# A second token half that starts with the weight blocks the first half ended with, and memory tokens transposed earlier

## The chip, the cores and the metric

The kernel runs on one core of one Trainium2 chip. The metric is the time of one execution on the device in microseconds. Five engines work side by side and meet through semaphores: TensorE (PE, with its weight loads as PEld), VectorE (DVE), ScalarE (ACT), GpSimd (POOL) and SyncE (SP), which here only issues the DMA transfers.

## The reference, cut to what matters

One decoder layer on 512 tokens of width 1024, all in float32. Four sub-layers, each wrapped in two RMS norms: a SwiGLU FFN, a token mixer, a cross-attention to 256 memory tokens, and a second FFN.

```
h = h + 0.5 * rmsnorm(swiglu(rmsnorm(h)))                      # FFN 1, width 2816
h = h + rmsnorm(concat(fox_attention, gla) @ w_out)            # mixer
q = rmsnorm(h) @ w_mq;  k, v = split(rmsnorm(mem) @ w_mkv)     # 4 heads of 256
o = softmax(q k^T / 16) v
h = h + rmsnorm(o @ w_mo)                                      # memory cross-attention
h = h + 0.5 * rmsnorm(swiglu(rmsnorm(h)))                      # FFN 2
```

The FoX attention has 8 heads of 64, the GLA part 4 heads in chunks of 64 tokens. The output of GLA is normed per head and gated.

## The kernel before, in words

**Products.** Every float32 product is made of three products of rounded parts: high x high, high x low, low x high (helper `three`, lines L1436, L1437, L1440). A weight block is 128 rows of 1024 values, 512 KB, or the same amount in another cut. SP fetches it into one of four slots (`raw`, L493), two transfers of 256 KB; ACT rounds it to its high part (`w_hi`, L644, in `round_block`/`round_to`); POOL subtracts to get the low part, in place of the raw block (`w_lo`, L588, in `split`); TensorE waits for the low part (`weights(n)`). SP may refill a slot when `w_used` says that the block four places earlier is finished. Blocks are numbered through the whole program: `B_OUT` begins the mixer's output weight, `B_MO` the memory output weight, `B_UP2` the second FFN.

**Row products.** A sub-layer's output is built in the eight PSUM banks: tile m is 128 tokens by 512 columns, tiles 0 to 3 are the first token half, 4 to 7 the second. `rows_block` adds one weight block to some tiles; `closing_rows` adds two blocks to each tile and so finishes the tiles one after another (`tile_done`, `w_used`). `rows_norm` on ACT (square, L691; root, L671) and DVE (sum of the two squares of a token row, L1060; weighing, L1062; `h`, L1073) norms the tiles and adds them to `h`. `turn_half` (L1513) then transposes `h` on TensorE, ACT and DVE write its high and low parts `xh` (L658) and `xl` (L1030), and `opening_pair` begins the next sub-layer with the first token half.

**Memory output.** The product with `w_mo` is made once for each token half: the first half inside the memory attention, as filling between its units, the second half after it. The eight blocks are fetched twice, 0 to 7 for each half, 16 block numbers from `B_MO`.

**Attention loops.** The FoX attention runs over 32 units (head, token tile), the memory attention over 16. In turn k TensorE makes the scores of unit k, the output of the pair that ends with unit k-3, and transposes the probabilities of unit k-2; ACT makes the exponential, then rounds weight blocks up to a number tied to the filling (`round_to`), copies out a finished output, copies the transposed probabilities (`pt_hi`, L861 and L897); DVE takes the maximum (L1209, L1211), normalises (L1140) and makes the low part (`pt_lo`, L1178 and L1220). Between these stands filling: `FILL` gives for each FoX turn how many quarters of a mixer input block TensorE puts in, `MEM_FILL` gives for each memory turn the number of items before and after the attention output. The first 16 items there are quarters of the last query blocks, the others the rows of the memory output; the last four are `closing_rows` items of two products each.

**GLA end.** After the last GLA output TensorE goes on to `fox_out(0..7)`, halves of the first four mixer output blocks, which need PSUM banks that ACT squares (L935) and DVE copies out (L1361). In between stand `sums` (L1921), the transposes of the memory tokens `mem_turn(0)` and `mem_turn(1)` (L1905), and `spread_head` (L1929), which waits for the reciprocal of the norm's root (L1363).

[...]

## Time and profile before

| | us |
|---|---|
| Median of 3 runs | 1189.07 (1186.98 to 1190.51) |
| The profiled execution's own time | 1188.42 |
| Its span in the profile | 1186.69 |
| TensorE busy in it | 1160.1 |
| ACT, POOL, DVE busy in it | 454.6, 499.4, 352.4 |

The times of rows in the next section count from the start of the span. In a row of the timeline stand: start, duration, engine, line, operation, output<-inputs, shapes, how many, and in brackets the time that the engine was idle before it and what ended that.

### The profile page before, as it was taken

The numbers are of one execution on the slowest core, as the hardware profiler recorded it, in microseconds if no ns is written. First come the engines' busy times: TensorE is split into PE (matmuls) and PEld (weight loads), VectorE is DVE, ScalarE is ACT, GpSimd is POOL, SyncE is SP. The second block draws the span as 40 slices with busy tenths as digits, with TensorE's granted clock in tenths as the row PEclk, the third lists the DMA queues.
The fourth block names the chain that finished last, engine by engine and source line by source line (L and its number), as shares of the span: only waits on it lengthen the run. The fifth ranks groups of instructions, "written<-read, shape, count | busy, mean of one in ns | idle before, by whom it ended". The sixth has DMA issues, their size and how long they took to land.

```text
span 1186.7 us, 15254 instructions
## 1 busy us (share of the span) xinstructions
PE 1160.1 (98%) x5664; PEld 965.5 (81%) x5664; DVE 352.4 (30%) x718; ACT 454.6 (38%) x744; POOL 499.4 (42%) x227
## 2 busy tenths in 40 slices
PE   8999999999999999999899999899999999999998
PEld 7888888888888778787778988778888888888886
DVE  2221311310006274655545204544122131130003
ACT  6232332322126455454535545456423233231213
POOL 5354354354443542222325754256434435435441
PEclk9999999999999999999999999999999999999999
DMA  6323333332322222111223442233332333323232
GB/s 201 105 91 99 96 94 101 92 103 89 106 89 71 89 89 72 54 54 43 83 69 109 160 142 89 73 126 107 104 105 90 98 96 92 103 89 106 89 107 107
DMA packets 86141, 115.13 MB, mean 97 GB/s; under 512 B 8974, under 2 KB 54092, under 8 KB 86092
## 3 DMA queue, kind: packets, MB, share of 16 engines
q1 hardware_dynamic: 86000, 114.44, 29.7%
q8 instruction: 33, 0.54, 0.2%
q14 instruction: 16, 0.13, 0.0%
q10 hardware_dynamic: 92, 0.02, 0.0%
HBM read 112.34 MB, written 2.10 MB: 96 GB/s over the span
## 4 chain that ended last, share of the span: by engine, by line
PE 61%; issue 24%; POOL 11%; DVE 2%; DMA 1%; ACT 1%; POOLq 0%; SPq 0%; DVEq 0%
PE bank L1436 20%; PE bank L1440 20%; PE bank L1437 20%; POOL w_lo L588 10%; PE bank L1477 1%; DVE h L1073 1%; DMA raw<-in_ffn_w_gu 1%; DVE bank L1062 0%; PE bank L1513 0%; POOL q_hi L626 0%; POOL q_lo L626 0%; DVE tmp L1062 0%; DVE f_ms L1060 0%; ACT w_hi L644 0%; ACT xh L658 0%
## 5 line engine op out<-in xcount | busy, mean ns | idle before, releaser
L588 POOL TENSOR_TENSOR w_lo<-raw,w_hi 128x1024 fp32r<-128x1024 f32 x204 | 488.3, 2403 | 665.0 <-ACT w_hi L644 664.3
L1436 PE MATMUL bank<-xh,w_hi 128*128 128x512 f32 (+1 forms) x912 | 349.8, 384 | 2.7 <-POOL w_lo L588 2.0
L1437 PE MATMUL bank<-xh,w_lo 128*128 128x512 f32 (+1 forms) x912 | 348.3, 382 | 0.0
L1440 PE MATMUL bank<-xl,w_hi 128*128 128x512 f32 (+1 forms) x912 | 348.3, 382 | 0.0
L644 ACT ACTIVATE w_hi<-raw 128x1024 fp32r<-128x1024 f32 x204 | 213.3, 1057 | 349.5 <-DMA raw<-in_ffn_w_down 167.5
L1436 PEld LDWEIGHTS bank<-xh,w_hi 128*128 128x128 f32 x912 | 171.5, 188 | 36.6 <-POOL w_lo L588 2.6
L1440 PEld LDWEIGHTS bank<-xl,w_hi 128*128 128x128 f32 x912 | 171.4, 188 | 33.6
L1437 PEld LDWEIGHTS bank<-xh,w_lo 128*128 128x128 f32 x912 | 171.5, 188 | 32.0
L1436 PE MATMUL bank<-w_hi,mid_hi 128*128 128x512 f32 x352 | 137.3, 390 | 0.0
L1440 PE MATMUL bank<-w_lo,mid_hi 128*128 128x512 f32 x352 | 137.0, 389 | 0.0
L1437 PE MATMUL bank<-w_hi,mid_lo 128*128 128x512 f32 x352 | 136.9, 389 | 0.0
L1107 DVE TENSOR_TENSOR tmp<-bank,rinv 128x512 f32<-128x512 f32 x44 | 30.2, 686 | 343.8 <-PE bank L1440 327.6
L753 ACT ACTIVATE tmp<-tmp 128x512 f32<-128x512 f32 x44 | 27.8, 633 | 152.0 <-DVE tmp L1107 152.0
L1436 PEld LDWEIGHTS bank<-w_hi,mid_hi 128*128 128x128 f32 x352 | 66.1, 188 | 14.1 <-DVE tmp L1108 0.6
L1440 PEld LDWEIGHTS bank<-w_lo,mid_hi 128*128 128x128 f32 x352 | 66.1, 188 | 13.9
L1437 PEld LDWEIGHTS bank<-w_hi,mid_lo 128*128 128x128 f32 x352 | 66.1, 188 | 13.6
L1436 PE MATMUL bank<-w_hi,xh 128*128 128x512 f32 x160 | 64.6, 404 | 3.3 <-POOL w_lo L588 2.9
L1440 PE MATMUL bank<-w_lo,xh 128*128 128x512 f32 x160 | 63.0, 394 | 0.0
L1437 PE MATMUL bank<-w_hi,xl 128*128 128x512 f32 x160 | 63.0, 394 | 0.0
L1062 DVE SCALAR_TENSOR_TENSOR bank<-bank,g_row 128x512 f32<-128x512 f32 x20 | 13.7, 693 | 135.4 <-ACT sq L691 135.4
L1062 DVE SCALAR_TENSOR_TENSOR tmp<-bank,g_row 128x512 f32<-128x512 f32 x12 | 8.1, 684 | 105.8 <-ACT sq L691 105.8
L1436 PEld LDWEIGHTS bank<-w_hi,xh 128*128 128x128 f32 x160 | 30.5, 190 | 10.4 <-issue 4.1
(232 smaller groups left out, 1211.6 us busy)
## 6 DMA issues: line engine op xcount, KB each, us to landing
raw<-in_ffn_w_gu SPq DMA_DIRECT2D x176, 256.0 KB, 2.9
raw<-in_ffn_w_down SPq DMA_DIRECT2D x88, 256.0 KB, 2.8
raw<-in_mix_w_in SPq DMA_DIRECT2D x48, 256.0 KB, 2.8
raw<-in_mem_w_kv SPq DMA_DIRECT2D x32, 256.0 KB, 3.1
raw<-in_mem_w_o SPq DMA_DIRECT2D x32, 256.0 KB, 2.9
raw<-in_mix_w_out SPq DMA_DIRECT2D x16, 256.0 KB, 3.0
raw<-in_mem_w_q SPq DMA_DIRECT2D x16, 256.0 KB, 2.9
h<-in_x SPq DMA_DIRECT2D x4, 512.0 KB, 5.3
```

The source lines that it names most:

```text
L588: gp.tensor_tensor(w_lo[:, n % SLOTS, :], raw[:, n % SLOTS, :], w_hi[:, n % SLOTS, :].bitcast(F32), ALU.subtract).then_inc(lo_ready, 1)
L644: act.activation(w_hi[:, n % SLOTS, :], raw[:, n % SLOTS, :], ACT.Copy).then_inc(hi_ready, 1)
L753: act.activation(tmp[:, pair, :], tmp[:, pair, :], ACT.Silu).then_inc(silu_done, 1)
L1062: dve.scalar_tensor_tensor(out=weighted_at(n)[:, :], in0=out_bank(s, n)[:, :], scalar=POST_SCALE[s], in1=g_row[:, cols], op0=ALU.mult, op1 ...
L1073: dve.scalar_tensor_tensor(out=h[:, t, cols], in0=weighted_at(n)[:, :], scalar=f_rinv[:, r], in1=h[:, t, cols], op0=ALU.mult, op1=ALU.add) ...
L1107: dve.tensor_tensor(tmp[:, pair, :], b[pair][:, :], rinv[:, :], ALU.mult).then_inc(gate_scaled, 1)
L1436: pe.matmul(dst, w[0], x[0], start=start, stop=False, skip_group_check=loose)
L1437: pe.matmul(dst, w[1], x[0], start=False, stop=False, skip_group_check=loose)
L1440: return pe.matmul(dst, w[0], x[1], start=False, stop=stop, skip_group_check=loose)
L1477: last = pe.matmul(bank[m][:, TOK[half]], slot[:, cols], x[:, c, TOK[half]], start=half == c == 0 and not low_w and not low_x, stop=False, ...
```

## The change

1. The second token half of the memory output begins with blocks 4 to 7, which still lie in the four slots when the first half is done, and then takes blocks 0 to 3. Twelve block numbers instead of 16: four fetches, roundings and splits fewer. `turn_half(3, 0)` stands after the fifth of the eight blocks (before: after the fourth, in this half's order).
2. The first half ends with single items instead of `closing_rows`; its last block's products finish the tiles (`tile_done`). `MEM_FILL` is dealt out anew.
3. In the memory attention ACT rounds after the `pt_hi` copy, not ahead of the output copy.
4. `FILL`: the last four entries 2, 2, 2, 2 become 2, 2, 2, 1, 1 with one turn more (the entries before it are as they were).
5. `mem_turn(0)` stands ahead of `fox_out(0)`.
6. The sum of two squares (L1060) is a `tensor_scalar` instead of a `tensor_tensor`.
7. ACT's roundings around the norm of the memory output are placed to fit.

```diff
-B_UP2 = B_MO + 2 * DC
+B_UP2 = B_MO + DC + KB
@@ FILL, last row
-        1, 1, 1, 2, 1, 1, 1, 2, 2, 2, 2)
+        1, 1, 1, 2, 1, 1, 1, 2, 2, 2, 1, 1)
@@ MEM_FILL
-MEM_FILL = ((3, 0), (2, 1), (1, 1), (1, 1), (1, 1), (1, 1), (1, 1), (0, 0), (1, 2), (2, 1),
-            (2, 1), (1, 1), (1, 1), (1, 2), (1, 2), (1, 2), (1, 2), (1, 0), (1, 1))
+MEM_FILL = ((3, 0), (2, 1), (1, 1), (1, 1), (1, 1), (1, 1), (1, 1), (0, 2), (0, 2), (1, 2),
+            (2, 1), (1, 1), (1, 1), (1, 1), (1, 2), (1, 2), (1, 2), (2, 1), (2, 2))
...
@@ ACT rows_norm
-                round_to(start + 1 if s != 2 else B_MO + DC + 2)
+                round_to(start + 1 if s != 2 else B_MO + DC)
                 act.preload_act_table(ACT.Sqrt)
                 for t in range(2):
                     square(t, 0)
                     square(t, 1)
                     root(t)
-                    if s == 2:
-                        round_to(B_MO + DC + 4 + 2 * t)
                 if s == 2:
-                    for q in range(2):
-                        half_hi(3, 0, range(4 * q, 4 * q + 4))
-                        round_to(B_UP2 - 1 + q)
+                    round_to(B_UP2 - 1)
+                    half_hi(3, 0, range(4))
+                    round_to(B_UP2)
+                    half_hi(3, 0, range(4, DC))
+                    round_to(start + 1)
                 round_to(start + 2)
@@ ACT mem_attention
-                    round_to(mem_block("q", 1, 0) + 3 + mem_blocks_used(MEM_FILLED[k]))
                     output(k - LATE - 1)
...
                                        ACT.Copy).then_inc(pt_h, 1)
+                    round_to(min(mem_block("q", 1, 0) + 3 + MEM_FILLED[k] // 4, B_MO + DC))
@@ DVE weigh
-                        dve.tensor_tensor(f_ms[:, t:t + 1], f_sq[:, n - 1:n], f_sq[:, n:n + 1],
+                        dve.tensor_scalar(f_ms[:, t:t + 1], f_sq[:, n - 1:n], f_sq[:, n:n + 1], None,
                                           ALU.add).then_inc(tile_sum, 1)
@@ PE mem_fill
-                    elif q < ROWS_Q:
+                    else:
                         c, m = (q - GROUP_Q) // 4, q % 4
                         if m == 0:
                             pe.wait_ge(y_l, mem_y(c, 0))
-                        rows_block(2, B_MO + c, (xh[:, c, :], xl[:, c, :]), c == 0,
-                                   free={m: (mq_l, 5 + m)} if c == 0 else {}, ms=(m,), used=m == 3)
-                    else:
-                        if q == ROWS_Q:
-                            pe.wait_ge(y_l, mem_y(DC - 2, 0))
-                        closing_rows(2, B_MO + DC - 2, [(xh[:, c, :], xl[:, c, :]) for c in (DC - 2, DC - 1)],
-                                     range(q - ROWS_Q, q - ROWS_Q + 1), TC)
+                        if c == 0:
+                            pe.wait_ge(mq_l, 5 + m)
+                        last = row_product(2, m, weights(B_MO + c), (xh[:, c, :], xl[:, c, :]), c == 0, c == DC - 1)
+                        if c == DC - 1:
+                            last.then_inc(tile_done, 1)
+                        elif m == TC - 1 and c < KB:
+                            last.then_inc(w_used, 1)
@@ PE gla
+                mem_turn(0)
                 fox_out(0)
                 fox_out(1)
                 fox_out(2)
                 sums().then_inc(gstat, 1)
-                mem_turn(0)
@@ PE memory
-                for ms in ((4, 5), (6, 7)):
-                    for c in range(2):
-                        pe.wait_ge(y_l, mem_y(c, 1))
-                        rows_block(2, B_MO + DC + c, (xh[:, c, :], xl[:, c, :]), c == 0, free={} if c else free,
-                                   ms=ms, used=ms[-1] == ROWS - 1)
-                for c in range(2, DC - 2):
+                for c in (*range(KB, DC), 0, 1):
+                    n = B_MO + (c if c >= KB else DC + c)
                     pe.wait_ge(y_l, mem_y(c, 1))
-                    rows_block(2, B_MO + DC + c, (xh[:, c, :], xl[:, c, :]), False, ms=range(TC, ROWS))
-                    if c == 3:
+                    rows_block(2, n, (xh[:, c, :], xl[:, c, :]), c == KB, free=free if c == KB else {},
+                               ms=range(TC, ROWS))
+                    if c == 0:
                         turn_half(3, 0)
-                closing_rows(2, B_MO + 2 * DC - 2, [(xh[:, c, :], xl[:, c, :]) for c in (DC - 2, DC - 1)],
-                             range(TC, ROWS))
+                closing_rows(2, B_UP2 - 2, [(xh[:, c, :], xl[:, c, :]) for c in (2, 3)], range(TC, ROWS))
```

## Rows read from the trace of the kernel before

**Rows 1.** The page, busy time, share of span and instructions of each engine
```profile
PE 1160.1 (98%) x5664; PEld 965.5 (81%) x5664; DVE 352.4 (30%) x718; ACT 454.6 (38%) x744; POOL 499.4 (42%) x227
```
**Rows 2.** Waits of TensorE, whole span: us in total, times, longest
```profile
PE bank L1436 <- POOL w_lo L588: 4.9, 5, 1.4
PE bank L1436 <- DVE pt_lo L1220: 2.9, 3, 1.8
...
PE bank L1436 <- DVE pt_lo L1178: 2.0, 2, 1.4
```
**Rows 3.** Timeline, end of the FoX attention
```profile
567.67 0.60 PE L1713 MATMUL bank<-ident,prob 128*128 128x128 f32 x4
569.68 0.50 PE L1436 MATMUL bank<-pt_hi,v_hi 128*128 128x512 f32 x1 [1.41 <-DVE pt_lo L1178]
...
568.93 0.69 DVE L1178 TENSOR_TENSOR pt_lo<-bank,pt_hi 128x512 fp32r<-128x512 f32 x1 [1.54 <-ACT pt_hi L861]
```
**Rows 4.** L1060 and L1211 (ns min/median/max, first and last start); timeline beside splits
```profile
L1060 DVE TENSOR_TENSOR f_ms<-f_sq x16: 150/152/1259, 364.6 to 1182.0; 128x1 f32<-128x1 f32 x16
L1211 DVE TENSOR_SCALAR nmx<-smax,rinv_tok x16: 212/215/217, 716.8 to 776.9; 128x1 f32<-128x1 f32 x16
...
815.88 2.38 POOL L588 TENSOR_TENSOR w_lo<-raw,w_hi 128x1024 fp32r<-128x1024 f32 x1 [2.12 <-ACT w_hi L644]
...
817.02 1.26 DVE L1060 TENSOR_TENSOR f_ms<-f_sq 128x1 f32<-128x1 f32 x1
...
765.16 1.20 DVE L1140 TENSOR_SCALAR prob<-prob,rr 128x256 f32<-128x256 f32 x1
```
**Rows 5.** Timeline, TensorE's first product of the mixer
```profile
374.33 0.35 PE L1436 MATMUL bank<-xh,w_hi 128*128 128x256 f32 x1 [0.58 <-DVE xl L1030]
```
**Rows 6.** Timeline, TensorE from the last GLA output to the spread
```profile
590.36 0.47 PE L1436 MATMUL bank<-w_hi,q_hi 128*128 128x512 f32 x1 [1.51 <-DVE gla_o L1361]
...
595.63 1.09 PE L1905 MATMUL bank<-ident,mem_n 128*128 128x128 f32 x8
...
599.89 1.98 PE L1929 MATMUL bank<-tmp,ident 128*128 128x512 f32 x4 [0.42 <-DVE tmp L1363]
```
**Rows 7.** Windows (stretch, its length, busy by engine, granted clock, DMA, GB/s); timeline, memory attention
```profile
743.00:749.10 6.10, 3.79 (x26) 3.07 (x25) 4.54 (x11) 2.81 (x6) 2.19 (x1) 1.00 0.24 86
749.10:752.50 3.40, 3.40 (x11) 2.72 (x11) 1.33 (x4) 1.21 (x4) 0.20 (x1) 0.50 0.00 0
...
745.79 1.04 ACT L644 ACTIVATE w_hi<-raw 128x1024 fp32r<-128x1024 f32 x1
...
747.62 0.39 PE L1436 MATMUL bank<-pt_hi,vm_hi 128*128 128x256 f32 x1 [1.81 <-DVE pt_lo L1220]
...
764.53 0.39 PE L1436 MATMUL bank<-pt_hi,vm_hi 128*128 128x256 f32 x1 [0.81 <-DVE pt_lo L1220]
...
778.94 0.39 PE L1436 MATMUL bank<-pt_hi,vm_hi 128*128 128x256 f32 x1 [0.23 <-DVE pt_lo L1220]
```
**Rows 8.** Timeline, ACT and TensorE around block 7 of the first half
```profile
778.32 1.05 ACT L644 ACTIVATE w_hi<-raw 128x1024 fp32r<-128x1024 f32 x1
...
783.87 0.38 ACT L897 ACTIVATE pt_hi<-bank 128x256 fp32r<-128x256 f32 x1 [2.60 <-PE bank L1765]
...
781.98 0.47 PE L1436 MATMUL bank<-w_hi,xh 128*128 128x512 f32 x1 [0.65 <-POOL w_lo L588]
```
**Rows 9.** Timeline, second token half and opening of the second FFN
```profile
789.47 0.39 PE L1436 MATMUL bank<-w_hi,xh 128*128 128x512 f32 x1
...
792.42 0.47 PE L1436 MATMUL bank<-w_hi,xh 128*128 128x512 f32 x1 [1.43 <-POOL w_lo L588]
...
815.85 0.28 PE L1436 MATMUL bank<-xh,w_hi 128*128 128x256 f32 x1
...
822.57 1.97 PE L1513 MATMUL bank<-ident,h 128*128 128x128 f32 x16 [1.11 <-DVE h L1073]
...
814.75 1.06 ACT L644 ACTIVATE w_hi<-raw 128x1024 fp32r<-128x1024 f32 x1 [3.46 <-DMA raw<-in_ffn_w_gu]
```

More of the change, by code:

```diff
@@ L156 @@
 MEM_Q_END = MEM_FILLED.index(GROUP_Q) - 1
-ROWS_Q = GROUP_Q + 4 * (DC - 2)
-assert MEM_FILLED[-1] == ROWS_Q + 4
-def mem_blocks_used(items):
-    return items // 4 if items < ROWS_Q else (ROWS_Q // 4 + (2 if items == ROWS_Q + 4 else 0))
+assert MEM_FILLED[-1] == GROUP_Q + 4 * DC
 PAIR_TURN = tuple(fill_turn(j, GROUP_Q - 2) for j in range(len(FILL_GROUPS)))
@@ L420, in wait_rows @@
         def wait_rows(eng, s, n):
-            if s == 2 and n == TC - 1:
-                eng.wait_ge(w_used, B_MO + DC)
-            elif n < ROWS - 1:
-                eng.wait_ge(tile_done, (ROWS - 1) * s - (s == 3) + n + 1 - (s == 2 and n >= TC))
+            if n < ROWS - 1:
+                eng.wait_ge(tile_done, (ROWS - 1) * s + n + 1)
             else:
@@ L1565, in row_product, with closing_rows @@
                              start, end, True)
-            def closing_rows(s, n, xs, ms=range(ROWS), end=ROWS):
+            def closing_rows(s, n, xs, ms=range(ROWS)):
                 ws = [weights(n), weights(n + 1)]
@@ L1572, in closing_rows @@
                         last = row_product(s, m, ws[k], xs[k], False, k == 1)
-                        if m == end - 1:
+                        if m == ROWS - 1:
                             last.then_inc(w_used, 1)
-                    if m < end - 1:
+                    if m < ROWS - 1:
                         last.then_inc(tile_done, 1)
```

## The prediction, on record before the change was run

> **What bounds the kernel now.** TensorE is busy 98% of the span [rows 1], so what can be won is its idle time and its time at a low clock. The view of waits gives the idle time by cause: 4.9 us on POOL's weight splits (five waits), 2.9 us on `pt_lo` in the memory attention, 2.0 us on `pt_lo` in the FoX attention [rows 2], and single ones of 1.5 us on the copies of the GLA output, 1.1 us on `h` and 0.6 us on `xl` [rows 5, 6, 9]. The reader is to see that these are a dozen short stops, each with its own releaser, and that the change touches the place of nearly all of them. So I went to each place in the timeline. Every edit is costed at the one stop it touches; where a stop goes, the engine is bound by its own work again and the shift travels on. A row product is three 512-column products, 0.68 us (four of them, a block of one token half, 2.73 us).
>
> **1. The last FoX turns (FILL).** Turn 33 held two quarters (1.37 us each), turn 34 none: after the transpose at 567.67 TensorE waits for `pt_lo` until 569.68 [rows 3]. Now one quarter goes behind the transpose. The transpose starts 1.37 us sooner (its `prob` is long normalised; the `pt_lo` before it ends at 566.20), its chain of 1.26 us to `pt_lo` runs beside the quarter. **-1.3 us**; bounds 0 (the chain is held by DVE, which has two evacuations at 566.12) and -1.4.
>
> **2. The sum of two squares (L1060).** It normally takes 0.15 us, but three of the 16 take 1.14 to 1.26 us, and those start while POOL splits a block and end with it (817.02 beside 815.88+2.38; 370.15 and 639.45 likewise) [rows 4]. The new form, one tile and a per-partition scalar, is that of L1211: 0.212 to 0.217 us in all 16 executions [rows 4], the one at 764.84 well inside a split that began at 763.82. So 1.0 us comes back per held sum, and 0.06 us is lost on every one. At 370 us the sum delays `h`, `xh` and `xl`: TensorE starts the mixer at 374.33 [rows 5] rather than at 373.59, and its second product waits 0.33 more, together 1.07 us. **-1.0 us** (0 to -1.1). The second held sum (639 us) has no stop of TensorE behind it; the third is in part 6. In the last stage no POOL split is near, and DVE runs without a gap through four tiles (2.79 us each, TensorE gives one in 2.73): four times 0.06, **+0.25 us** (0 to +0.3).
> The Trainium skill, "SBUF — State Buffer", section "Who interferes with whom", has a rule against this step: `tensor_scalar` is among the operations that can take the port pair shared with GpSimd, and then whoever comes second is fully blocked. Rows for the wide form agree: the normalising at 765.16 took 1.20 us beside a split, against 0.35 [rows 4]. The one-column form of L1211 shows no such hold, so the sum goes by the row. By the rule of the Trainium skill's page this part would be +0.06 us instead of -1.0 and the time 1181.4.
>
> **3. Memory tokens turned first (mem_turn).** Before, 8 transposes stood at 595.63 between the sums and `fox_out(3)`, 0.83 us. Ahead of `fox_out(0)` TensorE is idle anyway until 590.36, waiting for the GLA copies; the normalised tokens are ready at 588.67 and the last GLA product is issued at 588.74, so the transposes fit. But the 0.83 us saved behind the sums only makes TensorE reach the reciprocal earlier, where it already waits: 599.89 is set by ACT's root and DVE's 3.35 us [rows 6], which start from the sums, and those are not moved. **0**. Cover gone (tokens late), it costs 0.9; were the reciprocal early, it gains 0.8.
>
> **4. The memory attention.** Two edits. ACT now rounds a block (1.05 us) after the `pt_hi` copy instead of before it, and turns 7 and 8 are filled (0,2), (0,2) instead of (0,0), (1,2). At 745.79 the rounding stood ahead of the copy at 746.74; TensorE stood still till 747.62, 1.97 us after its last issue, and right after it the granted clock fell to 0.50 (1.2 GHz) from 749.10 to 752.50 [rows 7], 1.7 us lost at half speed. Now: the two products of turn 7 wait for `qm_lo` (744.05 and 744.7), transpose 5 starts at 745.45, its copy directly behind the exponential (745.9), `pt_lo` at 746.7, output 746.85, two more products, transpose 6 at 749.7 with one product more done than before at 751.77. That is 2.1 + 0.7 and a rest of 0.2 of the low clock: -3.0. The same reordering takes away the stop of 0.97 at 764.53, whose copy also stood behind a rounding, and two gaps of 0.3 and 0.1; the stop before 778.94 stays, since no rounding stands there [rows 7]. **-4.4 us** for the way to output 13 (before: 778.94), of it 1.7 the clock. Ends: -1.5 (the clock falls all the same and DVE's normalising is held by POOL, 0.85 at a time as at 765.16) and -4.8.
>
> **5. The last block of the first half.** Here the order works against the change. Block 7 was rounded at 778.32, ahead of output 13; still TensorE waited until 781.98 for POOL [rows 8]. Now its rounding stands behind the copy of transpose 14, which comes 2.83 us after output 13 starts (call that O): copy O+3.25, rounding O+3.53, split O+4.66 to O+7.06 (spacings as before: copy 783.87 [rows 8], rounding 784.15, split 785.28). TensorE has output 13 (1.45), products 39 to 43 and two transposes, and wants block 7 at O+5.2: a **new wait of 2.0 us**. The first half ends at O+11.4; before 789.47-778.94 = 10.53. **+0.9 us** (+0.2 to +1.5). Queued behind are output 15 and ACT's copy of it, on which the fourth product of the second half waits, covered by the five before it.
>
> **6. Second half and opening of the FFN.** Before 26.4 us from 789.47 to 815.85: 32 products 21.9, 16 transposes 1.7, the rest stops on POOL at 792.42 and 810.32 [rows 9]. Four loads (2 MB in eight transfers), four roundings and four splits go. Blocks 4 to 7 need no wait, 10.9 us of cover. Block 8's slot is free at 2.7, landed 3.6 later, split by 9.6, wanted at 10.9; 9 and 10 have more room. But the transposes of the first half's rows now come one block, not two, before the closing pair, and block 11 is rounded behind four `xh` copies: transposes at 13.7, rounding +2.1, split done +5.7, wanted +4.45: a wait of 1.3 (0.96 before). End at 24.95: **-1.4 us** (0 to -2.8).
> Opening: 6.7 us from 815.85 to the transposes at 822.57, of which 4.3 is work [rows 9]. ACT is held by the landing of the second FFN block (814.75), then come squares, the held sum, `h`. The landing now hangs on the end of the block before the closing pair, 6.9 us before the end instead of 6.5, and the sum isn't held: 4.3 to 5.5 us. **-1.8 us** (-1.2 to -2.4).
>
> **The sum.** -1.3 -1.0 +0.25 +0 -4.4 +0.9 -1.4 -1.8 = -8.75. Against the profiled execution (1188.42, span 1186.69) that is 1179.7; the median of the runs lies 0.65 higher, so 1180.3.
>
> **Rivals.**
> *The clock falls again.* The only fall inside the kernel followed a stop of 1.97 us; one of 1.6 us (before 792.42) brought none [rows 7, 9]. The new wait of part 5 is 2.0. Price 1.7: 1182.0. Chance 0.20.
> *The attention is bound by its chain.* A unit goes maximum, exponential, normalising, transpose, copy, low part; with TensorE ahead sooner, and wide normalising held by splits that start at other moments, part 4 gives only -1.5 and part 5 the +1.5: 1183.8, with part 6 small too 1186. Against it: from 749 to 779 TensorE's cadence is its own but for three stops. Chance 0.12.
> *The loads were hidden anyway.* 16 blocks to 12 does nothing, part 6 is 0: 1183.5. Against it two POOL stops stand in that half. Chance 0.04.
> *The sum stays held.* The new form, begun while a split runs, ends with the split as the old one did at 817.02, and as the wide scalar form did at 765.16; parts 2 and 6 lose up to 1.0 each: 1181.3 to 1182.3. Against it stand 16 executions of L1211 [rows 4]. Chance 0.05. (This is the rule of the Trainium skill's page "SBUF — State Buffer" in part 2.)
> *Slower.* Roundings behind `pt_hi` come late for blocks 3 to 6 as for 7. From copy to split is 4.2 us; the work between is about 6 us for those four, 2.2 for block 7. It decides against the change when the waits exceed 12.3 us in all, five blocks at 2.5: 1192.6. Chance 0.04.
>
> **Chances and range.** The forecast itself 0.55. 0.3% (3.6 us) is about what a measurement tells from no change, so below 1185.5 is faster: all but the slower case and most of the chain's bad end, 0.86; within 0.10; slower 0.04. The range runs from 1177.6 (best ends of parts 4 and 6) to 1185.0, into the chain-bound rival.
>
> **What the profile after would show.** FoX output 31 with no stop before it; every L1060 near 0.21 us; 8 transposes before 590 and a longer wait at the reciprocal; clock 1.00 throughout the memory stage; a wait of about 2 us on POOL one product pair before output 15; none at the start of the second half; 12 loads of 512 KB of the output weight; opening of 4.3 to 5.5 us. Wrong it would be if the clock falls elsewhere, or if a stop that I take to vanish moves behind the next releaser, as in part 3.

## The result, and the profile after

The changed kernel takes 1180.96 us (median of 5 runs, 1180.82 to 1181.41) against 1188.83 us (median of 5, 1186.98 to 1190.51): a ratio of 0.9935, 95% interval 0.9922 to 0.9948, so 7.9 us faster; 8.75 us and a median of 1180.3 us were forecast. Its profiled execution has a span of 1179.2 us against 1186.7. Two disturbed runs of one variant below (no_reuse, 1289.5 and 1448.5 us) and one of the kernel before (1662.4 us) are used nowhere. Lines from the attention on stand ten lower than in the kernel before (L1436 is now L1426, L1060 is L1050).

The page, busy time by engine, and the view of waits of TensorE (us in total, times, longest), kernel after:

```profile
PE 1158.5 (98%) x5664; PEld 965.3 (82%) x5664; DVE 356.3 (30%) x718; ACT 451.7 (38%) x740; POOL 489.9 (42%) x223
PE bank L1426 <- POOL w_lo L578: 3.9, 3, 1.7
...
PE bank L1426 <- DVE pt_lo L1210: 1.5, 3, 0.7
PE bank L1919 <- DVE tmp L1353: 1.2, 1, 1.2
...
PE bank L1426 <- DVE pt_lo L1168: 0.6, 1, 0.6
```

Beside [rows 1, 2]: four roundings and four splits are gone, and the waits on `w_lo` and on both kinds of `pt_lo` fell from 9.8 to 6.0 us. The busy sum fell by 1.6 us, about the 1.7 us that the half-speed stretch had cost (TensorE counted as busy for all of its 3.40 us [rows 7]); the rest of the gain is idle time.

Both kernels issue 5664 TensorE products, so the start of product number n can be compared in two traces; the difference, watched along the span, says at which place time is won or lost. Its steps, with the terms of the prediction (us, minus is faster):

| place | predicted | measured |
|---|---|---|
| opening of the mixer (part 2) | -1.0 | -0.82 |
| end of the FoX attention (part 1) | -1.3 | -1.29 |
| memory tokens turned first (part 3) | 0 | 0 |
| memory attention up to output 13 (part 4) | -4.4 | -2.99 |
| end of the first half (part 5) | +0.9 | +0.99 |
| second half (part 6) | -1.4 | -1.46 |
| opening of the FFN (part 6) | -1.8 | -2.48 |
| last stage (part 2) | +0.25 | +0.19 |

The steps not shown are +0.5 us before the first product that the change touches and -0.1 us near 643 us. All of them together give the 7.5 us by which the two spans differ.

L1050 over the whole span (ns min/median/max), and TensorE between the last GLA output and the spread, kernel after:

```profile
L1050 DVE TENSOR_SCALAR f_ms<-f_sq x16: 199/206/214, 365.1 to 1174.5; 128x1 f32<-128x1 f32 x16
```
```profile
587.20 1.06 PE L1895 MATMUL bank<-ident,mem_n 128*128 128x128 f32 x8
588.75 0.47 PE L1426 MATMUL bank<-w_hi,q_hi 128*128 128x512 f32 x1 [0.48 <-DVE gla_o L1351]
598.27 1.98 PE L1919 MATMUL bank<-tmp,ident 128*128 128x512 f32 x4 [1.25 <-DVE tmp L1353]
```

None of the 16 sums is held; beside [rows 4], whose longest took 1.26 us. Against [rows 6] the wait on `gla_o` fell from 1.51 to 0.48 and the one before the spread grew from 0.42 to 1.25: the transposes fit, and the gain ends at the reciprocal.

The clock by stretch, kernel after (length, busy by engine, granted clock):

```profile
743.00:749.10 6.10, 5.88 (x37) 5.01 (x36) 5.08 (x13) 3.51 (x8) 2.40 (x1) 1.00 0.03 11
749.10:752.50 3.40, 3.40 (x21) 2.87 (x20) 1.72 (x6) 1.65 (x4) 0.00 (x0) 1.00 0.48 154
```

The fall to 0.50 of [rows 7] isn't there. But part 4 gave 1.4 us less than forecast. By the products, turns 7 and 8 gave 2.6 us (3.0 forecast) and the stop that had been at 764.53 in the kernel before gave 0.95 (0.97 forecast); behind it 0.6 us was lost, where 0.4 was to be won. Timeline of the stretch where it is missing, kernel after (start, duration, in brackets the idle time before and its releaser):

```profile
760.04 2.40 POOL L578 TENSOR_TENSOR w_lo<-raw,w_hi 128x1024 fp32r<-128x1024 f32 x1 [4.73 <-ACT w_hi L634]
760.48 2.11 DVE L1130 TENSOR_SCALAR prob<-prob,rr 128x256 f32<-128x256 f32 x1
763.60 2.39 POOL L578 TENSOR_TENSOR w_lo<-raw,w_hi 128x1024 fp32r<-128x1024 f32 x1 [1.16 <-ACT w_hi L634]
764.37 1.77 DVE L1130 TENSOR_SCALAR prob<-prob,rr 128x256 f32<-128x256 f32 x1
766.53 0.39 PE L1426 MATMUL bank<-pt_hi,vm_hi 128*128 128x256 f32 x1 [0.66 <-DVE pt_lo L1210]
...
774.21 0.39 PE L1426 MATMUL bank<-pt_hi,vm_hi 128*128 128x256 f32 x1 [0.65 <-DVE pt_lo L1210]
...
777.55 0.38 ACT L886 ACTIVATE pt_hi<-bank 128x256 fp32r<-128x256 f32 x1 [1.01 <-PE bank L1755]
777.83 1.05 ACT L634 ACTIVATE w_hi<-raw 128x1024 fp32r<-128x1024 f32 x1
...
778.96 2.35 POOL L578 TENSOR_TENSOR w_lo<-raw,w_hi 128x1024 fp32r<-128x1024 f32 x1 [5.29 <-ACT w_hi L634]
...
781.46 0.47 PE L1426 MATMUL bank<-w_hi,xh 128*128 128x512 f32 x1 [1.66 <-POOL w_lo L578]
```

Two things are to be seen. The normalising that takes 0.35 us alone starts 0.4 and 0.8 us after a split and ends within 0.15 us of it: the rounding now stands behind `pt_hi`, so the split begins just when VectorE normalises the next unit. And block 7 does as part 5 said: copy at O+3.3, rounding O+3.6, split O+4.75 to O+7.1 (O is 774.21), and a stop of 1.66 us where 2.0 was forecast.

The second half and the opening, kernel after, for [rows 9]:

```profile
799.33 1.91 PE L1503 MATMUL bank<-ident,h 128*128 128x128 f32 x16
805.08 0.47 PE L1426 MATMUL bank<-w_hi,xh 128*128 128x512 f32 x1 [1.10 <-POOL w_lo L578]
...
807.81 1.06 ACT L634 ACTIVATE w_hi<-raw 128x1024 fp32r<-128x1024 f32 x1 [2.89 <-DMA raw<-in_ffn_w_gu]
808.78 0.58 ACT L681 ACTIVATE sq<-bank 128x512 f32<-128x512 f32 x1
```

Blocks 4 to 7 start without a wait, block 11 costs 1.10 us (forecast 1.3), and the opening takes 4.3 us from 810.64 to the transposes at 814.96, the work alone. In the kernel before the opening held two stops, and the prediction names one: that on `h` [rows 9]. The other, kernel before:

```profile
818.32 0.39 PE L1436 MATMUL bank<-xh,w_hi 128*128 128x256 f32 x1 [0.88 <-POOL w_lo L588]
```

Both are gone; by the products the first gave 1.1 us and the one on `h` 1.3. ScalarE still waits for the second FFN block, 2.89 us, but no longer on TensorE's path.

### The profile page after: what moved, and what is told of

It reads as the page before. It is cut to its first block, busy times and chain, and to the rows that moved or that the text cites. A ratio compares the mean times of both kernels' runs of the same rounds, so it can differ in the third digit from the quotient of the medians.

```text
span 1179.2 us, 15228 instructions
## 1 busy us (share of the span) xinstructions
PE 1158.5 (98%) x5664; PEld 965.3 (82%) x5664; DVE 356.3 (30%) x718; ACT 451.7 (38%) x740; POOL 489.9 (42%) x223
## 4 chain that ended last, share of the span: by engine, by line
PE 61%; issue 25%; POOL 11%; DVE 2%; DMA 0%; ACT 0%; POOLq 0%; SPq 0%; DVEq 0%
PE bank L1426 20%; PE bank L1427 20%; PE bank L1430 20%; POOL w_lo L578 10%; PE bank L1467 1%; DVE h L1063 1%; DMA raw<-in_ffn_w_gu 0%; POOL q_lo L616 0%; POOL q_hi L616 0%; DVE tmp L1052 0%; DVE bank L1052 0%; PE bank L1503 0%; ACT xh L648 0%; PE bank L1488 0%; PE bank L1445 0%
## 5 line engine op out<-in xcount | busy, mean ns | idle before, releaser
L578 POOL TENSOR_TENSOR w_lo<-raw,w_hi 128x1024 fp32r<-128x1024 f32 x200 | 478.8, 2404 | 666.8 <-ACT w_hi L634 666.0
L1426 PE MATMUL bank<-xh,w_hi 128*128 128x512 f32 (+1 forms) x912 | 349.7, 383 | 1.2 <-POOL w_lo L578 1.1
L634 ACT ACTIVATE w_hi<-raw 128x1024 fp32r<-128x1024 f32 x200 | 209.0, 1057 | 350.2 <-DMA raw<-in_ffn_w_down 167.5
L1426 PEld LDWEIGHTS bank<-xh,w_hi 128*128 128x128 f32 x912 | 171.5, 188 | 34.9 <-POOL w_lo L578 1.5
L1426 PE MATMUL bank<-w_hi,mid_hi 128*128 128x512 f32 x352 | 137.3, 390 | 0.0
L1426 PEld LDWEIGHTS bank<-w_hi,mid_hi 128*128 128x128 f32 x352 | 66.1, 188 | 14.3 <-DVE tmp L1098 0.6
L1426 PE MATMUL bank<-w_hi,xh 128*128 128x512 f32 x160 | 63.7, 398 | 3.8 <-POOL w_lo L578 2.8
L1426 PEld LDWEIGHTS bank<-w_hi,xh 128*128 128x128 f32 x160 | 30.1, 188 | 10.2 <-issue 3.5
```

The costliest lines, as they stand in the source:

```text
L578: gp.tensor_tensor(w_lo[:, n % SLOTS, :], raw[:, n % SLOTS, :], w_hi[:, n % SLOTS, :].bitcast(F32), ALU.subtract).then_inc(lo_ready, 1)
L634: act.activation(w_hi[:, n % SLOTS, :], raw[:, n % SLOTS, :], ACT.Copy).then_inc(hi_ready, 1)
L1426: pe.matmul(dst, w[0], x[0], start=start, stop=False, skip_group_check=loose)
```

## Experiments

The theory after the result: the terms are independent, each as priced, and only part 4 is over-priced, because the new order of ScalarE places the splits on the normalising. The rival: the clock and the turn sizes gave all of part 4, and the missing 1.4 us have another cause.

Each kernel is the changed one with one edit unless said otherwise. The columns are steps against the changed kernel at each place, in us from the starts of the same product in the profiled executions (+ is slower than the changed kernel), so they don't contain the differing starts of the executions (-0.5 to +1.4 us) that sit in the medians.

| kernel | median us | ratio to before (95%) | mixer opening | FoX end | attention | end of first half | second half | FFN opening |
|---|---|---|---|---|---|---|---|---|
| before | 1188.83 | | +0.82 | +1.29 | +2.99 | -0.99 | +1.46 | +2.48 |
| u_sum | 1182.50 | 0.9950 (0.9934-0.9967) | +0.82 | 0 | 0 | 0 | 0 | +0.68 |
| u_fill | 1182.33 | 0.9952 (0.9937-0.9968) | 0 | +1.31 | 0 | 0 | 0 | 0 |
| u_turn | 1181.23 | 0.9943 (0.9927-0.9960) | 0 | 0 | 0 | 0 | 0 | 0 |
| u_order | 1179.33 | 0.9926 (0.9905-0.9947) | 0 | 0 | +0.45 | -1.89 | 0 | 0 |
| early7 | 1179.53 | 0.9925 (0.9908-0.9942) | 0 | 0 | 0 | -1.89 | 0 | 0 |
| turn7 | 1180.93 | 0.9937 (0.9920-0.9954) | 0 | 0 | 0 | 0 | -1.16 | +1.06 |
| both | 1178.93 | 0.9921 (0.9906-0.9935) | 0 | 0 | 0 | -1.89 | -1.13 | +0.70 |
| b_order | 1186.33 | 0.9987 (0.9977-0.9997) | +0.82 | +1.29 | +0.47 | -0.99 | +1.50 | +2.33 |
| split4 | 1180.14 | 0.9934 (0.9917-0.9951) | 0 | 0 | -1.14 | 0 | 0 | 0 |
| norm_acc | 1179.66 | 0.9933 (0.9916-0.9949) | 0 | 0 | -1.18 | 0 | 0 | 0 |
| no_reuse | | | 0 | 0 | -0.53 | -0.85 | +1.51 | +1.06 |
| best | 1177.49 | 0.9916 (0.9902-0.9929) | 0 | 0 | -1.23 | -1.89 | -1.05 | +0.88 |

Entries of 0 are within 0.05. no_reuse has two usable runs, 1182.34 us (the profiled one) and 1181.12, and so no median here.

### Undoing one part at a time

**u_sum**

```diff
-    dve.tensor_scalar(f_ms[:, t:t + 1], f_sq[:, n - 1:n], f_sq[:, n:n + 1], None,
+    dve.tensor_tensor(f_ms[:, t:t + 1], f_sq[:, n - 1:n], f_sq[:, n:n + 1],
```

> The changed kernel with its sum of squares a tensor_tensor again (f_ms = f_sq + f_sq at line 1050); nothing else is undone. Theory (GpSimd's splits hold the tensor_tensor and not the tensor_scalar): some of the sixteen sums take 1.5 us and more again where they take 0.2 us in the changed kernel, TensorE's opening of the output mixer comes 0.8 us later against its matmuls, the opening of the second feed-forward network up to 0.9 us later, and the last stage gives 0.2 us back: 1.0 to 1.6 us slower than the changed kernel, 1182.0 to 1182.6 us. Rival (the gain at the two openings came from other edits, the roundings and the row schedule): the sums stay at 0.2 us and the time within 0.3 us.

Timeline of VectorE and GpSimd, then of TensorE, kernel u_sum:

```profile
370.69 1.15 DVE L1050 TENSOR_TENSOR f_ms<-f_sq 128x1 f32<-128x1 f32 x1
369.42 2.40 POOL L578 TENSOR_TENSOR w_lo<-raw,w_hi 128x1024 fp32r<-128x1024 f32 x1 [6.40 <-ACT w_hi L634]
...
811.07 1.29 DVE L1050 TENSOR_TENSOR f_ms<-f_sq 128x1 f32<-128x1 f32 x1
809.94 2.41 POOL L578 TENSOR_TENSOR w_lo<-raw,w_hi 128x1024 fp32r<-128x1024 f32 x1 [1.50 <-ACT w_hi L634]
```
```profile
374.88 0.36 PE L1426 MATMUL bank<-xh,w_hi 128*128 128x256 f32 x1 [0.59 <-DVE xl L1020]
```

Both sums end within 0.02 us of the split, and the stop of [rows 5] is back. The theory holds: 1.5 us slower, 0.82 at the mixer and 0.68 at the FFN. The rival, that this gain came from other edits, is out.

**u_fill**

```diff
-        1, 1, 1, 2, 1, 1, 1, 2, 2, 2, 1, 1)
+        1, 1, 1, 2, 1, 1, 1, 2, 2, 2, 2)
```

> The changed kernel with the old last entry of FILL (one turn with two quarters in place of two turns with one). Theory: the end of the FoX attention comes 1.3 us later against the matmuls before it and nothing behind it gives it back, 1.3 us slower, 1182.2 us. Rival (the wait at the spread of the gates takes up the lateness, because the chain on VectorE behind it is not moved): under 0.5 us.

Timeline of TensorE, kernel u_fill:

```profile
569.32 0.50 PE L1426 MATMUL bank<-pt_hi,v_hi 128*128 128x512 f32 x1 [1.41 <-DVE pt_lo L1168]
```

The stop of [rows 3] is back, +1.31 us, and it is never given back.

**u_turn** moves the line `mem_turn(0)` back behind `sums()`.

> The changed kernel with the first memory turn behind the sums again. Theory: nothing between the two places is short of a result, so the order alone costs nothing: within 0.2 us in the stage, and the wait before the spread of the gates falls from 1.25 back to about 0.4 us. Rival one (the earlier turn takes the stop before the third output block away): 0.4 us slower. Rival two (it makes the statistics late): 0.8 us faster.

Timeline of TensorE, kernel u_turn:

```profile
588.93 0.47 PE L1426 MATMUL bank<-w_hi,q_hi 128*128 128x512 f32 x1 [1.51 <-DVE gla_o L1351]
...
598.49 1.98 PE L1919 MATMUL bank<-tmp,ident 128*128 128x512 f32 x4 [0.42 <-DVE tmp L1353]
```

Both waits of [rows 6] are back to the hundredth, and all products from the spread on start within 0.05 us of where they would: this edit is worth nothing. Both rivals are out.

**u_order**

```diff
+                    round_to(min(mem_block("q", 1, 0) + 3 + MEM_FILLED[k] // 4, B_MO + DC))
                     output(k - LATE - 1)
...
                                        ACT.Copy).then_inc(pt_h, 1)
-                    round_to(min(mem_block("q", 1, 0) + 3 + MEM_FILLED[k] // 4, B_MO + DC))
```

> The changed kernel with ScalarE's block roundings ahead of its output copies and of the rounding of the turned probabilities, as before; the new row schedule stays. Theory: GpSimd then splits a block earlier in each turn, so the 128x256 normalising of the probabilities is held less (0.4 to 0.7 us in place of up to 2.1 us) while the turned probabilities come 1.2 us later; block 7 is rounded earlier and the 1.66 us stop at the end of the first half goes. The stops of turns 7 and 8 grow by 1.0 to 1.3 us each; the two changes meet within 1 us: 1180.0 to 1182.0 us. If the order is worth what I gave it, 1.8 us, and the block's wait only 0.9, the kernel is 0.9 us slower. Rival (the order is of no account, only the turn sizes are): turns 7 and 8 unchanged, 1.7 us faster.

Timeline of TensorE, kernel u_order:

```profile
746.38 0.39 PE L1426 MATMUL bank<-pt_hi,vm_hi 128*128 128x256 f32 x1 [0.94 <-DVE pt_lo L1210]
...
761.71 0.39 PE L1426 MATMUL bank<-pt_hi,vm_hi 128*128 128x256 f32 x1 [0.82 <-DVE pt_lo L1210]
```

The old order costs 0.70 us at turn 7 and 0.95 more by 765 us, then wins 1.20 back up to output 13 and 1.89 at block 7: 1.4 us faster than the changed kernel. So the mechanism was right in each place, but the order's net worth was not: once the turns are filled, the new order of ScalarE is a net loss over the attention and block 7 together. The clock stayed at 1.00 without it. The old order's gain behind 765 us fits less hold on the normalising (mean 441 ns, below).

**b_order** is the kernel before with the rounding moved behind `pt_hi` in the first eleven turns, nothing else.

```diff
-                    round_to(mem_block("q", 1, 0) + 3 + mem_blocks_used(MEM_FILLED[k]))
+                    if k > 10:
+                        round_to(mem_block("q", 1, 0) + 3 + mem_blocks_used(MEM_FILLED[k]))
                     output(k - LATE - 1)
...
                                        ACT.Copy).then_inc(pt_h, 1)
+                    if k <= 10:
+                        round_to(mem_block("q", 1, 0) + 3 + mem_blocks_used(MEM_FILLED[k]))
```

> The kernel before with one edit: in the first eleven turns of the memory attention ScalarE rounds the next block behind the rounding of the turned probabilities and not ahead of the output copy. Theory: the turned probabilities of turns 7 and 8 come 1.2 us earlier, TensorE's two stops of 2 us there shrink under 1 us each, and the granted clock does not fall to 0.50 from 749.1 to 752.5 us: 3.5 us faster than before. Rival one (the stop still trips the clock, since no products fill the turns): 1.8 us faster with the clock at 0.50. Rival two (the order is of no account, the moved row products are): no change in the two stops and in the time.

In the kernel before, ScalarE started the copy only as the rounding ahead of it ended (745.79 to 746.83 in [rows 7]):

```profile
746.74 0.37 ACT L897 ACTIVATE pt_hi<-bank 128x256 fp32r<-128x256 f32 x1
```

Timeline of TensorE, and the clock by stretch, kernel b_order:

```profile
747.16 0.39 PE L1439 MATMUL bank<-pt_hi,vm_hi 128*128 128x256 f32 x1 [0.86 <-DVE pt_lo L1223]
```
```profile
743.00:749.10 6.10, 4.74 (x32) 3.97 (x31) 4.94 (x14) 3.42 (x8) 1.43 (x1) 1.00 0.25 86
749.10:752.50 3.40, 3.40 (x20) 2.87 (x20) 2.15 (x3) 1.35 (x4) 0.97 (x1) 1.00 0.05 17
```

The stop fell from 1.81 us [rows 7] to 0.86 and the clock stayed at 1.00 (2.4 GHz). In the profiled executions that is 2.5 us less up to output 13, about 0.95 from the stop and the rest from the clock; the second stop, at 762.50, kept its 0.81. The runs on one chip show only 1.2 us (1187.56 to 1186.33). So either edit by itself brings the stop of turns 7 and 8 under 1 us, and in the one profiled execution of each no slow stretch followed: the order here, the filling in u_order.

The mean granted clock of every run says more. In the profiled executions of the changed kernel and its variants the clock is at half speed only in the last 0.5 to 4 us, and the means of 51 of their 52 runs are 0.998 to 1.0 (the other is split4's profiled one, 0.95). Of the 40 later runs of the kernel before, ten have 0.996 or 0.997, and of the ten of b_order five have 0.997. A mean of 0.997 is 6 to 8 us at half speed (an estimate: 0.0025 to 0.0035 of 1185 us, doubled), more than that end. So the clock most likely fell inside half of b_order's runs as well; where, and after what stop, no trace shows. Only with the turns filled is there no such run. And the kernel before does not fall in each execution: its 11 runs at 0.999 or 1.0 have a median of 1186.75 us, the other 29 one of 1188.25, and the 1.5 us between them are near the 1.7 us that the slow stretch cost in its profile.

### Where the missing 1.4 us went

**split4**

```diff
+                if B_MO + 2 <= n < B_MO + 7:
+                    gp.wait_ge(hi_ready, n + 1)
+                    for j in range(0, BW, 128):
+                        ins = gp.tensor_tensor(w_lo[:, n % SLOTS, j:j + 128], raw[:, n % SLOTS, j:j + 128],
+                                               w_hi[:, n % SLOTS, j:j + 128].bitcast(F32), ALU.subtract)
+                    ins.then_inc(lo_ready, 1)
...
```

> The changed kernel with the low parts of five blocks of the memory output (blocks 2 to 6 of the first half) computed by GpSimd in four instructions of 128 columns each in place of one of 512. The work is the same. 
(A block is 1024 columns wide, so it is eight instructions of 128 in place of one of 1024, not four in place of one of 512.)

**norm_acc**

```diff
...
+    if u >= N_FOX:
+        dve.tensor_scalar(prob[:, u % PROBS, 0:w], prob[:, u % PROBS, 0:w], rr[:, r], None,
+                          ALU.mult, ALU.add, accum_out=junk[:, r]).then_inc(normed, 1)
+        return
...
```

> The changed kernel with the normalising of the memory attention's probabilities as a tensor_scalar that also accumulates its sum (into a column that nothing reads). Theory: the plain tensor_scalar runs two elements at a time and is the one held by GpSimd; with the sum it runs at the slower rate, 0.5 to 0.6 us in place of 0.35 us free, but is not held: no instruction over 0.8 us, the attention up to output 13 0.8 to 1.4 us shorter. Rival (it is held whatever its form): the longest stay near 2 us and the time is equal or 0.3 us longer.

The view of lines, VectorE from 735 to 785 us (busy us, mean ns of one), in the kernels after, u_order, split4 and norm_acc:

```profile
L1130 DVE TENSOR_SCALAR prob<-prob,rr 128x256 f32<-128x256 f32 x12 | 11.1, 928 | 0.4
```
```profile
L1130 DVE TENSOR_SCALAR prob<-prob,rr 128x256 f32<-128x256 f32 x12 | 5.3, 441 | 0.4
```
```profile
L1143 DVE TENSOR_SCALAR prob<-prob,rr 128x256 f32<-128x256 f32 x12 | 6.5, 541 | 0.4
```
```profile
L1132 DVE TENSOR_SCALAR_CACHE_REDUCE prob<-prob,rr 128x256 f32<-128x256 f32 x12 | 5.7, 479 | 0.4
```

The same stretch of TensorE, the stop before output 13, kernels split4 and norm_acc:

```profile
773.90 0.38 PE L1439 MATMUL bank<-pt_hi,vm_hi 128*128 128x256 f32 x1 [0.24 <-DVE pt_lo L1223]
```
```profile
772.83 0.38 PE L1431 MATMUL bank<-pt_hi,vm_hi 128*128 128x256 f32 x1 [0.23 <-DVE pt_lo L1215]
```

Two edits on different engines give the same gain at the same place, 1.14 and 1.18 us: the stop near 766.5 goes and the one before output 13 falls from 0.65 to 0.23. In norm_acc each normalising of the memory attention takes 478 to 480 ns, slower than the free 350, and none is held. In split4 the longest from 745 us on takes 0.68 us, though GpSimd is busy 3.5 us with a block in eight pieces against 2.4 in one. So VectorE held by GpSimd cost the changed kernel 1.2 us here, all of it behind 765 us, where 1.0 of the missing 1.4 us lay. The Trainium skill, "SBUF — State Buffer", section "Who interferes with whom", names `tensor_scalar` as an operation that can take the shared port pair and excepts the form that also writes its accumulator; both halves of that agree with these rows (2.11 us held, 0.48 never). The prediction told the first half as a rule against its part 2; but the same section makes that hold depend on conditions that the operands must meet, and it has a `tensor_tensor` with two inputs in SBUF contend with a GpSimd instruction that reads SBUF, which u_sum agrees with (1.15 and 1.29 us on one column). split4 as a whole gained less: 0.5 us was lost between 571 and 735 us, ahead of the pieces. GpSimd's loop was written out for it; that this is the reason was not shown.

**no_reuse** is the kernel before with all edits except the shared blocks: both halves load eight blocks, the old end of the first half and, but for one item less in turn 16, the old turn sizes from turn 11 on stay. The part of its diff on the sizes:

```diff
-        1, 1, 1, 2, 1, 1, 1, 2, 2, 2, 2)
+        1, 1, 1, 2, 1, 1, 1, 2, 2, 2, 1, 1)
-MEM_FILL = (... (1, 1), (0, 0), (1, 2), (2, 1), (2, 1), (1, 1), (1, 1), (1, 2), (1, 2), (1, 2), (1, 2), ...)
+MEM_FILL = (... (1, 1), (0, 2), (0, 2), (1, 2), (2, 1), (1, 1), (1, 1), (1, 2), (1, 2), (1, 2), (1, 1), ...)
...
```

> The kernel before with every edit but the reuse of blocks: the FILL end, the first memory turn, the tensor_scalar sum, ScalarE's order and the turn sizes of the memory attention's turns 7 to 10; both halves still load eight blocks each (sixteen in all) and the old end of the first half stays. Theory: it has the gains of the parts 1, 2 and 4 of the prediction (1.3 + 1.4 + 3.0 us at the places measured) without block 7's stop (0.9) and without the shorter second half and opening (1.4 + 2.4): 1183.0 us, 5.5 us faster than before, 2.0 to 3.0 us slower than the changed kernel. Rival (the reuse is where the gain comes from, through the loads): 1186 us and more.

Timeline of TensorE, kernel no_reuse:

```profile
777.05 0.47 PE L1436 MATMUL bank<-w_hi,xh 128*128 128x512 f32 x1 [0.90 <-POOL w_lo L588]
...
787.49 0.47 PE L1436 MATMUL bank<-w_hi,xh 128*128 128x512 f32 x1 [1.39 <-POOL w_lo L588]
```

Its last product starts 1.2 us later than that of the changed kernel, start aside, and not 2 to 3 as expected: the reuse of the blocks, which the change is named for, brings 1.5 us in the second half and 1.1 at the opening. What came with it in the first half, the new end and the turn sizes from turn 11 on, costs 1.4. The other edits bring the rest: over six of the 7.9 us.

### Mending what is left

**early7** and **turn7**

```diff
-    round_to(min(mem_block("q", 1, 0) + 3 + MEM_FILLED[k] // 4, B_MO + DC))
+    round_to(min(mem_block("q", 1, 0) + 3 + MEM_FILLED[k] // 4 + (k == 15), B_MO + DC))
```
```diff
-                    if c == 0:
+                    if c == DC - 1:
                         turn_half(3, 0)
```

> The changed kernel with one more block rounded in turn 15 (ScalarE rounds block 7 of the first half one turn earlier). Theory: the stop of 1.66 us on block 7's low part at the end of the first half goes, nothing else takes it over: 1.5 to 1.8 us faster than the changed kernel, 1179.3 us. Rival one (the rounding then waits for the block's load and holds the turned probabilities behind it): the stop moves to the last turns, less than 0.5 us gained. Rival two (the second half meets its own wait, the rounding queue is one block short everywhere): gained at 785 us, given back by 811 us.

> The changed kernel with the transposes of the last rows' half moved from behind the fifth block of the second half (c = 0) to behind the fourth (c = 7). Theory: block 11's low part, on which TensorE stands 1.10 us, waits behind ScalarE's or GpSimd's order; with the transposes ahead of it the stop of 1.1 us shrinks by their 1.0 us, and their own wait does not grow: 0.5 to 1.2 us faster. Rival (the transposes wait for the rounded rows, which are not there one block earlier): equal or up to 1 us slower.

**both** has the two edits together.

> The two edits early7 and turn7 together, on the changed kernel. Theory: they lie in different halves, so their gains add: 2.0 to 3.0 us faster than the changed kernel, 1178.0 to 1179.0 us. Rival: the stop of the second half depends on when block 7 is released (one queue of slots), so the sum of both is that of the larger alone, 1.7 us.

ScalarE in early7, then TensorE and ScalarE in turn7, from the timelines:

```profile
773.19 0.38 ACT L886 ACTIVATE pt_hi<-bank 128x256 fp32r<-128x256 f32 x1 [0.24 <-PE bank L1755]
773.47 1.05 ACT L634 ACTIVATE w_hi<-raw 128x1024 fp32r<-128x1024 f32 x1
```
```profile
811.97 0.39 PE L1426 MATMUL bank<-xh,w_hi 128*128 128x256 f32 x1 [0.49 <-POOL w_lo L578]
...
808.38 1.06 ACT L634 ACTIVATE w_hi<-raw 128x1024 fp32r<-128x1024 f32 x1 [2.11 <-DMA raw<-in_ffn_w_gu]
809.35 0.58 ACT L681 ACTIVATE sq<-bank 128x512 f32<-128x512 f32 x1
```

early7: the block had landed, the rounding starts at once, the 1.66 us stop is gone and nothing takes it over, -1.89 us. It ran in turn 15, behind that turn's `pt_hi`, and held nothing up. turn7: block 11's stop goes, -1.16 us, and 1.06 come back at the opening, since the second FFN block lands no earlier: TensorE waits for its split (0.49 us) and the squares stand behind its rounding. Neither theory nor rival had that. The two edits add as expected (both), but what turn7 adds is small: 0.1 us alone and 0.4 in both, by the products.

**best** is norm_acc, early7 and turn7 with one new edit in `rows_norm`:

```diff
-                round_to(start + 2)
+                if s != 2:
+                    round_to(start + 2)
                 square(2, 0)
                 square(2, 1)
                 root(2)
+                round_to(start + 2)
```

> The changed kernel with the three edits that each measured a gain at its place, norm_acc (1.17 us in the memory attention), early7 (1.80 us at the end of the first half) and turn7 (1.15 us in the second half, of which 1.06 us came back at the opening of the second feed-forward network), and one new edit against what came back: ScalarE rounds the second weight block of that network behind the squares of the third token tile and not ahead of them, because in turn7 the squares stood behind a rounding that waited for its load. Theory (the places are independent): 3.0 us from the first two and 0.1 to 1.1 us from the rest, 1177.0 to 1178.0 us. Rival one (the late rounding makes the second block's low part late at the opening): the opening loses over 1 us, 1178.5 us. Rival two (the two edits of the first half share one wait): 1.8 us, 1179.1 us.

Timelines of ScalarE and of TensorE, kernel best:

```profile
804.54 0.30 ACT L662 ACTIVATE f_root<-f_ms,eps_t 128x1 f32<-128x1 f32 x1 [0.28 <-DVE f_ms L1053]
804.74 1.05 ACT L635 ACTIVATE w_hi<-raw 128x1024 fp32r<-128x1024 f32 x1
...
808.31 0.38 PE L1433 MATMUL bank<-xh,w_hi 128*128 128x256 f32 x1 [0.63 <-POOL w_lo L579]
```

1177.49 us (1177.29 to 1178.22), 3.5 us below the changed kernel, in the forecast interval: the gains of the attention (1.23), of block 7 (1.89) and of the second half (1.05) are all there. The new edit did not pay: the rounding no longer waits for the load, but it now comes late for TensorE, 0.63 us at 808.31, as rival one had it, and the opening loses 0.88 us where it lost 0.70 in the kernel both.

## Why the prediction was right

It was right in direction and nearly in size, and the mechanisms it names are what the runs confirm. The total is off by 0.9 us (7.9 against 8.75) where part 4 alone is off by 1.4, since the opening of the FFN gave 0.7 us more than forecast: so much of the nearness is luck. **Parts 1 and 2**: undone alone they cost 1.31 and 0.82 us, at the places named; one sum at the FFN is worth 0.68. **Part 3**, 0: undone, it costs nothing, and both waits swap as described. **Part 5**, +0.9: measured +0.99, and early7, where the stop is gone, shows that the late rounding was its cause. **Part 6**, second half: -1.4 against -1.46.

**The mis-sized term is part 4**, -4.4 against -2.99. Its step "the same reordering takes away the stop of 0.97 at 764.53" was true, but the sentence that named the held normalising kept it as an end of the range, at 0.85 us a time, and left it out of the value taken. The roundings were moved in the sum without moving what they start: the splits, which then fell on the normalising for up to 1.76 us beyond its 0.35. Without the hold this stretch is 1.2 us shorter (norm_acc, split4). The 0.4 us missing at turns 7 and 8, 2.6 for 3.0, isn't settled.
The text also credited the -3.0 at turns 7 and 8 to order and filling jointly. b_order and u_order show that either brings the stop that the slow clock followed under 1 us. With the filling there, the new order wins 0.70 us at turns 7 and 8 and 0.95 at the next stop, loses 1.20 behind that and 1.89 at block 7: a net loss of 1.4 us.

**The opening** gave 2.48, not 1.8. u_sum accounts for 0.68 of it and no_reuse for 1.06. The other 0.7 lies between the kernel before and these two, by the products: the stop on the second FFN block's low part is 1.1 us there and 0.7 in no_reuse, and the one on `h` 1.3 us there and 0.3 in no_reuse. So the held sum costs 1.0 us where the load is late, against 0.68 where it isn't (u_sum): the two causes do not simply add. That a late load uses up the slack ahead of the sum would explain it, but was not tested by itself. turn7 shows that the opening hangs on the landing of the second FFN block against the end of the row products, as the prediction had it.

**The rivals.** The clock did not fall again in the changed kernel: the new stop measured 1.66 us, not 2.0, and 1.00 was granted after it. The attention bound by its chain was partly true (the held normalising) and worth 1.2 us, not 2.9. The loads were not hidden: with the reuse the second half is 1.5 us shorter (no_reuse). The sum didn't stay held: 199 to 214 ns in all 16. The late roundings decided nothing outside block 7.

## What to carry to other kernels

Where an edit moves an instruction, price what that instruction starts as well: here a rounding moved by one copy put its split on top of another engine's work and ate most of what the move had won. Of two edits for one stop, test each alone; either may be enough for it, and the second may be a loss. And where a stop is taken off a stretch whose end hangs on a load, the time comes back at that load (turn7). The mean clock of all runs can show what one profile can't: whether a slow stretch comes each time.

## What the runs showed of the hardware

The granted clock fell to 0.50 after the stop of 1.81 us in the kernel before, with TensorE busy 3.79 of the 6.1 us up to the fall [rows 7]; in the other profiled executions stops of 0.86 us (b_order, 4.74 of 6.1 us), 0.94 us (u_order) and 1.66 us (after) brought none. An fp32 `tensor_scalar` on one column is not held by a GpSimd split (199 to 214 ns), a `tensor_tensor` on one column is (1.15 and 1.29 us), and a `tensor_scalar` on 256 columns is held until the split ends (2.11 us), unless it accumulates (480 ns at most). The runs of the kernel before lie 5.6 us apart (1185.5 to 1191.1), those of the changed kernel 0.6, those of its variants up to 2.1 and those of b_order 2.5. The slow stretch comes in some executions and not in others, as far as the mean clock shows it: the mean granted clock was 0.996 or 0.997 in 10 of 40 runs of the kernel before and in 5 of 10 of b_order, and below 0.998 in none of the changed kernel's and only one of its variants' (split4, 0.95 in its profile from 8 us to the last 4, with no product delayed by more than 0.02 us from 830 to 1170 us).
